# A three-layer forward pass in one kernel: where the delta net's chunk matrices and first inverses stand among the gate blocks

## The reference, cut to what matters

```python
m = jnp.where(strict, jnp.einsum('nbhik,nbhjk->nbhij', kb, kc) * decay, 0.0)
t_mat = lax.linalg.triangular_solve(eye + m, ..., lower=True, unit_diagonal=True)
u_base = jnp.einsum('nbhij,nbhjv->nbhiv', t_mat, vb)
w_mat = jnp.einsum('nbhij,nbhjk->nbhik', t_mat, kb * jnp.exp(gcum)[..., None])
qk = jnp.einsum('nbhik,nbhjk->nbhij', qc, kc) * decay
q_dec = qc * jnp.exp(gcum)[..., None]
...
o = _rms_f32(o) * norm_w * jax.nn.silu(gate)      # and the same kind of gate for the retention
```

## Time and profile before

| | |
|---|---|
| median of 3 runs | 1962.77 us (1962.27 to 1963.08) |
| the profiled execution's own time | 1960.69 us |
| its span, first to last instruction | 1958.9 us |
| TensorE busy | 1891.2 us, 97% |
| VectorE busy | 1220.4 us, 62% |
| ScalarE busy | 797.5 us, 41% |
| DMA queue of the weights | 24.6% of 16 engines' span |
| mean granted TensorE clock | 0.984 |

### The profile page before, as it was taken

The page is one execution under the profiler, slowest core; times in us unless marked ns, Lnnn a source line. Parts: engine busy times, 40 slices in busy tenths (PEclk is TensorE's granted clock), DMA queues, the critical chain, the costliest instruction groups (busy, mean ns, idle before and its releaser), DMA issues.

```text
span 1958.9 us, 21827 instructions
## 1 busy us (share of the span) xinstructions
PE 1891.2 (97%) x8620; PEld 1532.1 (78%) x8620; DVE 1220.4 (62%) x1750; ACT 797.5 (41%) x1286; POOL 0.2 (0%) x4
## 2 busy tenths in 40 slices
PE   8999899999999999988799999999999899999999
PEld 6766789788888888755588888888788688888887
DVE  5566666577777444635477777533988667777521
ACT  4137410454444333234454444323755554444311
POOL 0000000000000000000000000000000000000000
PEclk9999999999999999997899999999999999999999
DMA  6211110232222233210032232223111032222222
GB/s 225 86 54 65 49 28 1 64 120 97 97 97 95 90 96 117 92 32 17 28 124 97 97 98 94 100 93 101 54 44 54 11 108 97 97 97 97 94 95 80
DMA packets 48918, 160.69 MB, mean 82 GB/s; under 512 B 5552, under 2 KB 6192, under 8 KB 48688
## 3 DMA queue, kind: packets, MB, share of 16 engines
q1 hardware_dynamic: 48816, 159.29, 24.6%
HBM read 157.17 MB, written 2.10 MB: 81 GB/s over the span
## 4 chain that ended last, share of the span: by engine, by line
PE 90%; ACT 5%; DVE 4%; issue 1%; DMA 0%; DVEq 0%; SPq 0%; ACTq 0%
PE bank L156 89%; ACT mixer_arena L625 2%; ACT wh L625 1%; DVE mixer_arena L1040 1%; DVE mixer_arena L1048 1%; DVE even_arena L1534 1%; DVE wl L1040 1%; ACT even_arena L625 0%; PE bank L516 0%; DVE even_arena L1044 0%; ACT L625 0%; DVE even_arena L1048 0%; ACT conf_diag_l L625 0%; ACT conf_diag_h L625 0%; ACT sq L625 0%
## 5 line engine op out<-in xcount | busy, mean ns | idle before, releaser
L625 ACT ACTIVATE wh<-raw 128x1024 fp32r<-128x1024 f32 (+2 forms) x310 | 308.9, 999 | 790.0 <-PE bank L156 777.1
L156 PE MATMUL bank<-nh,wh 128*128 128x512 f32 x1520 | 602.4, 396 | 11.4 <-DVE nl L1048 8.2
L156 PE MATMUL bank<-nh,wl 128*128 128x512 f32 x1520 | 593.2, 390 | 0.0
L156 PE MATMUL bank<-nl,wh 128*128 128x512 f32 x1520 | 592.9, 390 | 0.0
L1040 DVE TENSOR_TENSOR wl<-raw,wh 128x1024 fp32r<-128x1024 f32 (+2 forms) x310 | 355.7, 1148 | 287.3 <-ACT wh L625 286.5
L156 PEld LDWEIGHTS bank<-nh,wh 128*128 128x128 f32 x1520 | 286.2, 188 | 76.6 <-DVE wl L1040 8.5
L156 PEld LDWEIGHTS bank<-nl,wh 128*128 128x128 f32 x1520 | 286.2, 188 | 63.3 <-issue 4.3
L156 PEld LDWEIGHTS bank<-nh,wl 128*128 128x128 f32 x1520 | 286.0, 188 | 60.3
L156 PE MATMUL bank<-ff_yh,wh 128*128 128x512 f32 x528 | 205.4, 389 | 0.0
L156 PE MATMUL bank<-ff_yl,wh 128*128 128x512 f32 x528 | 205.4, 389 | 0.0
L156 PE MATMUL bank<-ff_yh,wl 128*128 128x512 f32 x528 | 205.4, 389 | 0.0
(11 more groups left out here) (191 smaller groups left out, 1802.5 us busy)
## 6 DMA issues: line engine op xcount, KB each, us to landing
raw<-in_ff_a_up SPq DMA_DIRECT2D x44, 512.0 KB, 3.3
raw<-in_ff_b_up SPq DMA_DIRECT2D x44, 512.0 KB, 3.2
raw<-in_ff_c_up SPq DMA_DIRECT2D x44, 512.0 KB, 3.2
raw<-in_w_in SPq DMA_DIRECT2D x32, 512.0 KB, 3.3
raw<-in_pw SPq DMA_DIRECT2D x24, 512.0 KB, 3.3
raw<-in_even_in SPq DMA_DIRECT2D x16, 512.0 KB, 3.3
raw<-in_ff_a_down_a SPq DMA_DIRECT2D x8, 512.0 KB, 3.2
raw<-in_ff_a_down_b SPq DMA_DIRECT2D x8, 512.0 KB, 3.2
```

The costliest lines, as they stand in the source:

```text
L156: return e.matmul(out, lhsT, rhs, start=start, stop=stop, skip_group_check=True)
L625: return e.activation(out, in_, func, **kw).then_inc(n.give(sem), 1)
```

## The change

The groups of chunk t follow block t + 2 instead of block t + 1, on PE and on DVE. The flips of chunks 0 and 1 move from behind block 6 to behind block 7. Those of chunks 2 and 3 move from behind block 7 to behind the half block. On DVE the four `qd` multiplications move from in front of the first inverses of chunks 0 and 1 to behind those of chunks 2 and 3. ACT's and SP's programs are the same.

```diff
+    def flips(*chunks):
+        e.wait_ge(c.chunk_used, 4 * TB)
+        for t in chunks:
+            e.wait_ge(c.first_T, t + 1)
+            four(2 + t, lambda h, o: e.transpose(o, m1.T[:, t, hs[h]], c.ident[:, :])).then_inc(n.give(c.flipped), 1)
+
     for i in range(8):
         take(i % 2)
         piece(i % 2, c.nh, c.nl, range(DK))
-        if 1 <= i <= TB:
-            t, cs = i - 1, slice((i - 1) * P, i * P)
+        if 2 <= i <= TB + 1:
+            t, cs = i - 2, slice((i - 2) * P, (i - 1) * P)
...
-        if i >= 6:
-            e.wait_ge(c.chunk_used, 4 * TB)
-            for t in ((0, 1) if i == 6 else (2, 3)):
-                e.wait_ge(c.first_T, t + 1)
-                four(2 + t, lambda h, o: e.transpose(o, m1.T[:, t, hs[h]], c.ident[:, :])).then_inc(n.give(c.flipped), 1)
+        if i == 7:
+            flips(0, 1)
 
 
     down_slices(0, m1.yrh, m1.yrl, c.ret_low, 0)
+    flips(2, 3)
     vacate(0)
     vacate(1)
@@ vector_program
             tt(c.sq[:, (i - 1) % 2, :], c.sq[:, (i - 1) % 2, :], m1.oret[:, i - 1, :], ALU.mult, c.ret_mix)
-            chunk(i - 1)
+        if 2 <= i <= TB + 1:
+            chunk(i - 2)
         if i == TB:
             ret_low(2)
         if i == TB + 1:
             ret_low(3)
             settle()
-            for h in range(HEADS):
-                tt(m1.qd[:, h, :], m1.qd[:, h, :], m1.gq[:, h, :], ALU.mult, c.vec_step)
             e.wait_ge(c.mask_ready, 32)
-            settle()
             first_inverse(0)
             first_inverse(1)
         if i == TB + 2:
             first_inverse(2)
             first_inverse(3)
+            for h in range(HEADS):
+                tt(m1.qd[:, h, :], m1.qd[:, h, :], m1.gq[:, h, :], ALU.mult, c.vec_step)
```

## The result

The changed kernel took 1951.99 us in the median of five runs (1950.45 to 1952.53), and the kernel before 1962.39 (1961.03 to 1963.08, five runs). The ratio is 0.9946, with a 95% interval of 0.9932 to 0.9961. So it is faster, by 10.4 us. The steps near the change came out almost to the tenth. What was missing was 1 us in the profiled execution, gained in a part of the program that the change doesn't touch, and 0.6 us in the distance from that execution to the median.

The account below looks back on a forecast made before the run. PE's pauses and slow stretches were taken as the bound: 5.5 + 2.4 + 2.6 + 0.8 = 11.3 us, less 0.8 (flips) and 1.2 (qd), gives 9.3. So 1960.69 becomes 1951.4, plus 2.1 is 1953.5; range 1952.2 to 1956.3.

Parts of the forecast that it names:

- What bounds the kernel: Whole kernel: PE is busy 97% of the span, so time comes from PE's pauses and slow stretches.
- Part 1: Before chunk 0: block 2 fills PE's 5.76 us pause, removing 5.5 us of later work and saving 2.4 in clock.
- The clock term: At chunk 0: with the pause cut to 0.3 us it runs at full clock, 2.7 us for 5.1, 2.4 saved.
- rival D: Level chain starts at half clock after a 1.4 us PE pause; over the whole chain 53 us more, 2007; chance 0.02.
- Part 2: From chunk 0 to block 7: PE runs without waits, and block 7 ends at 257.2, 10.4 us earlier.
- Part 3: Behind block 7: DVE and ACT decide; block 7 scaled at 258.5, the product needing the first mask at 265.2.
- Part 4: Level chain: PE bounds its 59.2 us, its work is unchanged, and everything after follows its earlier start.
- rival A: Clock falls anyway, at chunk 0 or a later place: 2.4 us back, gain 6.9, 1955.9; chance 0.10.
- the 2.1: Whole kernel: the median of the runs was taken to lie 2.1 us above the profiled execution.
- `qd` term: On DVE before block 7's scaling: the qd multiplications queued ahead delay it by 1.2 us.
- B: DVE becomes the bound one round earlier, block 7's scaling comes 1.5 us later: gain 7.8, 1955.0; chance 0.09.
- C: Block 2 finds its weights or bank late and doesn't fill the pause: gain 3.8, 1959.0; chance 0.03.

Follow-up runs that it names:

- warm pause: The kernel before, with 24 spare products (results never read) filling PE's pause behind block 1; median 1960.57 us, ratio 0.9988.
- after again: The changed kernel measured once more with no edit; median 1952.66 us, ratio 0.9949 against the kernel before.
- late feed: The changed kernel, with DVE splitting the next piece behind the second mask instead of in front of the first; 1948.24 us in one run.
- chunks only: The kernel before, with only the chunks' groups moved one block back, flips and qd multiplications left in place; median 1956.04 us, ratio 0.9965.
- heads first: The kernel before, with DVE scaling the heads before it splits the next piece in round 0; median 1953.89 us, ratio 0.9954.

## Why the prediction was right near the change, and short at the lower end

- **What bounds the kernel**: right. The pause, the half clock and the flips between blocks were PE's time, and it came back but for what the chain over ACT kept.
- **Part 1, block 2 in the pause**: right. The pause left is 0.35 us (0.3 worked out). The clock term was 2.2 us alone in the warm pause, for 2.4. But the row that it leaned on was one execution's. Behind the same pause of 2.35 us (2.37 in after again) the clock was at half (0.50) in six of the fourteen traces; rows of one stand at the end of this section. So that pause was not free in each execution, and rival D's "cost nothing" holds for eight of the fourteen.
- **Part 2, to the end of block 7**: 257.31 for 257.2. No bank wait and no wait for `first_T`. DVE's slack before round 6 was 0.35 us for 0.4.
- **Part 3**: block 7 scaled at 258.46 (258.5), the first masked product at 265.17 (265.2), PE's wait 1.25 (1.4). The late feed shows that DVE's split in front of the mask causes this wait. That block 7's scaling stands behind `qd` the trace shows (over at 257.31, scaled at 258.46); what the `qd` multiplications cost in all was not run, only that another place for them saves 0.5 us.
- **Part 4, the level chain and what comes behind**: the chain is 59.2 us as before. This part failed in its last sentence, "everything after follows it". In the first pair of traces the attention stretch gave another 0.96 us, through the place where its clock fell. I had this as a loss only: rival A names "a later place that shifts against what grants the clock", and gives it 2.4 us against me. The warm pause shows that such a stretch can get shorter with no chunk moved (134.73), and the other traces of after that the gain can be 0.2 us as well (135.5).
- **How the numbers follow**: the forecast was 1951.4 for the profiled execution, and 2.1 from there to the median. The step that failed is in two terms of this sum. The first is what comes behind the level chain, put at nothing ("everything after follows it"). The gain was 9.29 us at the residual add behind the chain (342.03 to 332.74), for 9.3, and 10.24 in the profiled execution (1960.69 to 1950.45): the 0.95 between them is the attention stretch's 0.96. The second is the 2.1. The median of five stands 1.54 above the profiled execution, and that of before 1.70 (1962.39), not the 2.08 of three runs. Together this is 0.95 + 0.56 = 1.5 us, and the lower end of the range stood only 1.3 below the forecast, for the `qd` term alone. (1953.5 less the 1.2 of `qd` is 1952.3; the text has 1952.5.) How much of the 0.96 is in the median is not known, since only one of the five executions was traced, and it was the fastest. The same kernel's second median, 1952.66, lies within the range. A miss by 0.2 is thus within what two sets of runs of one kernel differ by (0.7), and so would a hit have been.
- **Rivals**: B and C did not occur. D did not either; the run with only the chunks moved had a fall of its kind, worth 1.7 us.

Open: the three further traces of after had two short stretches at half clock near 141 and 175, where nothing was changed, and scaled block 0 2.2 to 2.7 us later (210.3 to 210.8) than its first (208.10). In after again the two cost 1.6 us (from the product at 139.00 to that at 157.47, 18.47 us for 16.90) and 1.0 us (from 175.36 to the scaling of block 0, 34.96 for 33.96). These are the rows at 175 in after again, and the one at the same pause in the first trace of after:

```profile
175.36 1.65 PE L156 MATMUL bank<-mixer_arena 128*128 128x256 f32 x4 [2.37 <-DVE mixer_arena L1044]
175.36:178.36 3.00, 3.00 (x8) 2.53 (x9) 2.49 (x4) 1.83 (x3) 0.00 (x0) 0.50 0.00 1
```

```profile
174.14 0.92 PE L156 MATMUL bank<-mixer_arena 128*128 128x256 f32 x4 [2.36 <-DVE mixer_arena L1044]
```

Three other kernels had them too (chunks only, warm pause, heads first), and the three traces of before, the first of after and the other four kernels had none. The near stretch starts behind them and leaves them out. So its 9.7 is not what the traces gain in all: at the add behind the level chain the means of before and after (342.74 and 334.50) are 8.2 apart. I take it for the clock's scatter between executions, and did not test it.

## What to carry to other kernels

If an engine pauses because the next work isn't ready, look first for what the slower engine stands in. Here a split that waited for ACT kept DVE from work that was ready. Putting it later in the queue in one place gave 7.7 us of the near stretch on the kernel before, where moving whole groups of matrices gave 9.4. A second place gave another 1.3 on the changed kernel. The two without the moved groups were not run together. A chain over several engines is priced from its first wait to the next product, with every operation queued in front of it. In a kernel that has sparse stretches, the clock can fall in another place from one execution to the next. Here that made one stretch up to 0.8 us shorter or longer for the same kernel, and two falls elsewhere cost 2.6 us. A range needs such an amount on both sides, and the scatter of the base beside it; one trace of a short pause at full clock doesn't show that this pause is free.

## What the runs showed of the hardware that was not expected

- A pause of 5.8 us cost 2.2 us in clock beside itself (warm pause), but pauses of 1.1 and 0.6 us close together could bring the half clock as well (chunks only: 0.66 in the window behind them), while 0.8 and 0.6 at the same flips did not in the three traces of before and in that of heads first.
- Behind one and the same pause of 2.3 to 2.4 us the clock was at full speed in eight traces and at half in six, in four traces of one kernel once full and three times half.
- One stretch of the same 504 products took 134.3 to 135.7 us. The long ones (135.5 to 135.7) were those in which the clock fell 110.5 to 111.4 us in and was at half for 23.9 us; with a fall up to 110.0 or from 111.7 on, it was at half for 17.1 to 20.5 us and the stretch was about 1 us shorter.
